# Two projection units moved among the y products, four copies moved to ScalarE, and the last group's norm applied behind its out products

## The reference

```
proj = rmsnorm(h) @ w_in                      # z, xbc, dt
xbc  = silu(dwconv5(proj_xbc))                # x, B, C
y    = scan_forward(x,B,C) + scan_backward(x,B,C) + x * d_skip
y    = y * silu(z)                            # gate
yg   = y in 4 groups of 512 channels
yg   = yg * rsqrt(mean(yg*yg) + 1e-6)         # norm of one group
h    = h + (yg * norm_w) @ w_out
```

## Time and profile before

| what | value |
|---|---|
| median of 3 runs | 1836.99 us (1836.5 to 1837.8) |
| the profiled execution's own time | 1833.54 us |
| its span, first to last instruction | 1831.8 us |
| PE busy | 1578.1 us, 86% |
| DVE busy | 1282.2 us, 70% |
| ACT busy | 781.0 us, 43% |
| POOL busy | 165.6 us, 9% |
| TensorE clock granted, mean | 0.907 |

### The profile page before, as it was taken

One profiled execution on the slowest core, in us unless ns is written; L12 is line 12 of the kernel. 1 busy time (PEld: TensorE's weight loads), 2 busy tenths in 40 slices (PEclk: granted clock), 3 DMA queues, 4 the chain that ended last, 5 costly groups with the idle time before them and its releaser, 6 DMA issues.

```text
span 1831.8 us, 20798 instructions
## 1 busy us (share of the span) xinstructions
PE 1578.1 (86%) x7275; PEld 1269.4 (69%) x7275; DVE 1282.2 (70%) x1673; ACT 781.0 (43%) x1323; POOL 165.6 (9%) x200
## 2 busy tenths in 40 slices
PE   3984987987985799999998777887898999999996
PEld 1753756755754588778877556887686888888875
DVE  4577766866875676696679898997466677663355
ACT  3348465473473455513442322221234555542242
POOL 1153000000000450000001020000010000000000
PEclk7987998998997899999999986675899999999998
DMA  2233313303320523252334564662232323333231
GB/s 71 82 92 117 92 46 115 105 33 118 112 70 23 114 87 97 81 184 92 102 133 161 191 240 143 162 166 53 66 104 70 102 92 100 95 97 104 90 94 64
DMA packets 189607, 190.57 MB, mean 104 GB/s; under 512 B 47566, under 2 KB 178206, under 8 KB 185438
## 3 DMA queue, kind: packets, MB, share of 16 engines
q1 hardware_dynamic: 168926, 187.52, 32.4%
q10 hardware_dynamic: 20608, 2.10, 0.9%
HBM read 165.27 MB, written 24.31 MB: 103 GB/s over the span
## 4 chain that ended last, share of the span: by engine, by line
PE 59%; DVE 25%; ACT 9%; issue 4%; DMA 2%; ACTq 1%; SPq 1%; DVEq 0%
PE ring L1829 19%; PE ring L1830 18%; PE ring L1831 18%; ACT rows L992 3%; ACT rows L1002 3%; DVE w_lo L1224 2%; DVE rb L1631 2%; DMA rows<-log_decays 1%; DVE ul L1238 1%; PE pe_y L1972 1%; DVE cc L1348 1%; DVE s_prod L1590 1%; DVE tab L1551 1%; DVE ytmp L1502 1%; DVE rstd L1247 1%
## 5 line engine op out<-in xcount | busy, mean ns | idle before, releaser
L879 ACT ACTIVATE w_hi<-w_raw 128x1024 fp32r<-128x1024 f32 (+1 forms) x233 | 239.9, 1029 | 656.7 <-PE ring L1831 626.2
L1829 PE MATMUL ring<-uh,w_hi 128*128 128x512 f32 (+1 forms) x1160 | 461.9, 398 | 36.5 <-DVE w_lo L1224 30.1
L1830 PE MATMUL ring<-ul,w_hi 128*128 128x512 f32 (+1 forms) x1160 | 455.7, 393 | 0.0
L1831 PE MATMUL ring<-uh,w_lo 128*128 128x512 f32 (+1 forms) x1160 | 455.0, 392 | 0.0
L1224 DVE TENSOR_TENSOR w_lo<-w_raw,w_hi 128x1024 fp32r<-128x1024 f32 (+1 forms) x233 | 278.0, 1195 | 188.4 <-ACT w_hi L879 188.2
L1829 PEld LDWEIGHTS ring<-uh,w_hi 128*128 128x128 f32 (+1 forms) x1160 | 220.1, 190 | 94.7 <-DVE w_lo L1224 25.7
L1830 PEld LDWEIGHTS ring<-ul,w_hi 128*128 128x128 f32 (+1 forms) x1160 | 220.1, 190 | 47.3 <-issue 2.1
L1831 PEld LDWEIGHTS ring<-uh,w_lo 128*128 128x128 f32 (+1 forms) x1160 | 219.7, 189 | 47.4 <-issue 0.6
L1829 PE MATMUL ring<-gh,w_hi 128*128 128x512 f32 x480 | 190.5, 397 | 29.2 <-DVE w_lo L1224 16.1
L1830 PE MATMUL ring<-gl,w_hi 128*128 128x512 f32 x480 | 189.1, 394 | 0.0
L1831 PE MATMUL ring<-gh,w_lo 128*128 128x512 f32 x480 | 189.0, 394 | 0.0
(11 more groups left out here) (250 smaller groups left out, 2173.9 us busy)
## 6 DMA issues: line engine op xcount, KB each, us to landing
w_raw<-in_ffn_w_up SPq DMA_DIRECT2D x88, 512.0 KB, 3.5
w_raw<-in_ffn_w_down SPq DMA_DIRECT2D x40, 512.0 KB, 3.5
w_raw<-in_ssd_w_in SPq DMA_DIRECT2D x32, 512.0 KB, 4.4
rows<-log_decays SPq DMA_DIRECT2D x16, 1024.0 KB, 5.9
s_tables<-tab SPq DMA_DIRECT2D x16, 1024.0 KB, 6.2
slot<-s_tables SPq DMA_DIRECT2D x16, 1024.0 KB, 7.4
w_raw<-in_ssd_w_out SPq DMA_DIRECT2D x16, 512.0 KB, 3.5
w_raw<-in_ple_w_gate SPq DMA_DIRECT2D x16, 512.0 KB, 3.5
```

The costliest lines, as they stand in the source:

```text
L879: act.activation(w_hi[u % 2][:, 0:n], w_raw[:, u % 2, 0:n], ACT.Copy).then_inc(hi_done, 1)
L1829: pe.matmul(o, wh[:, k, c], rh[:, k0 + k, :], start=first and k == 0, stop=False)
L1830: pe.matmul(o, wh[:, k, c], rl[:, k0 + k, :], start=False, stop=False)
L1831: mm_ = pe.matmul(o, wl[:, k, c], rh[:, k0 + k, :], start=False, stop=last and k == nk - 1)
```

## The change

1. **Units of the next group among the y** (PE). In g = 0, 1 and 2 the two first xbc units of group g+1 are multiplied inside the y stage of g instead of behind it: the list `between` gives what stands ahead of `transposes(hp+1)` (or, for hp = 3, ahead of `outputs(3)`), and what stands after the last `outputs`. The second of the two units stands behind `outputs(3)` and ahead of `group_square(g)`. The loop over xbc of groups 1 to 3 begins with its third unit.
2. **x and B copies on ACT**. The four `xseq` copies and the `bseq` copy go from DVE to ACT, behind `hi_to(z + 3)` and ahead of the silu of z.
3. **The last group** (g = 3). y times `norm_w` alone is split into `yh_last` and `yl_last` inside the y stage, pair by pair: DVE `y_normed` and `y_rest`, ACT `y_hi` behind the decays that are due in that step. Its own out products follow without the norm; `group_square` comes after the first of them, and each pair of result tiles is multiplied by `ytmp` into a buffer `part` and then added to `h` (`take_last_out`: four DVE instructions in place of two). The out units 2 and 3 of group 2 move later in the y stage (`between[3]`), with their `hi`, `lo` and `take_out`.

```diff
--- before.py
+++ after.py
@@ -176,6 +176,10 @@
         bseq = sb("bseq", [P, SB, P], where=ssd)
         cb_fwd = sb("cb_fwd", [P, SEQ], where=ssd)
         zs = sb("zs", [P, GT, SEQ], where=ssd)
+        last_y = ExitStack()
+        yh_last = sb("yh_last", [P, GT, SEQ], F32R, last_y)
+        yl_last = sb("yl_last", [P, GT, SEQ], F32R, last_y)
+        last_y.close()
         xd = sb("xd", [P, 2, GC], where=ssd)
         car = sb("car", [P, 2, SB - 1, GC], where=ssd)
         yo = sb("yo", [P, SB, GC], where=ssd)
@@ -196,6 +200,7 @@
         speq = rows_[0][0:2 * HEADS, 0, 0, :]
         cs_row = rows_[1][0:2 * HEADS, 0, 0, :]
         ssd.close()
+        YH, YL = [yh] * (GROUPS - 1) + [yh_last], [yl] * (GROUPS - 1) + [yl_last]
 
         def ffn_memory(layer, where):
             m = ExitStack()
@@ -361,6 +366,7 @@
         y5_skip, y5_gelu = sem("s5_skip_added"), sem("s5_gelu")
         g5_hi, g5_lo = sem("g_hi"), sem("g_lo")
         glu_sig, glu_mul = sem("glu_sigmoid"), sem("glu_product")
+        out_scaled = sem("out_scaled")
         hn_done = sem("h_normed")
         stored = sem("output_stored")
 
@@ -969,6 +975,12 @@
                         act.wait_ge(taps, 8 * (3 * g + i) + 6 + j + 1)
                         act.activation(dst, cc[:, q % 4, :], ACT.Silu).then_inc(silu, 1)
                 hi_to(z + 3)
+                for c in range(SB + 1):
+                    name, k = (("xseq", g), c) if c < SB else (("bseq", g), 0)
+                    act.wait_ge(evac, T[name] + k)
+                    act.wait_ge(filled, FILL[name] + k + 1)
+                    dst = xseq[:, c, :] if c < SB else bseq[:].rearrange("p c n -> p (c n)")
+                    act.activation(dst, bank(T[name] + k), ACT.Copy).then_inc(evac, 1)
                 for i in range(2):
                     if i == 1:
                         if g == 0:
@@ -1006,10 +1018,19 @@
                 if g:
                     hi_to(w + 2)
                 decays(1)
+                def y_hi(m):
+                    act.wait_ge(yn_done, GT * g + m + 1)
+                    act.activation(YH[g][:, m, :], zs[:, m, :], ACT.Copy).then_inc(yh_done, 1)
+
                 for hp in range(GT + 1):
                     if hp + 2 < GT:
                         decays(hp + 2)
-                    if hp + 1 < GT and g:
+                    if g == GROUPS - 1:
+                        if hp:
+                            y_hi(hp - 1)
+                        if hp in (0, 2, 4):
+                            hi_to(w + 3 + hp // 2)
+                    elif hp + 1 < GT and g:
                         hi_to(w + hp + 3)
                     if hp >= 1:
                         n = GT * g + hp - 1
@@ -1023,11 +1044,10 @@
                 act.activation(var[:], var[:], ACT.Sqrt).then_inc(gstd, 1)
                 if g < GROUPS - 1:
                     hi_to(U[("xbc", g + 1)] + 2)
-                if g:
-                    act.wait_ge(unit_done, w + 4)
-                for m in range(GT):
-                    act.wait_ge(yn_done, GT * g + m + 1)
-                    act.activation(yh[:, m, :], zs[:, m, :], ACT.Copy).then_inc(yh_done, 1)
+                    if g:
+                        act.wait_ge(unit_done, w + 4)
+                    for m in range(GT):
+                        y_hi(m)
             for i in range(4):
                 hi_to(U[("out", GROUPS - 1)] + i + 2)
                 for m in (2 * i, 2 * i + 1):
@@ -1372,10 +1392,7 @@
                 take_z(0)
                 lo_to(z + 3)
 
-                for c in range(SB):
-                    take(("xseq", g), c, xseq[:, c, :])
-                dve.wait_ge(filled, FILL[("bseq", g)] + 1)
-                dve.tensor_copy(bseq[:], bank(T[("bseq", g)]).rearrange("p (c n) -> p c n", c=SB)).then_inc(evac, 1)
+                dve.wait_ge(evac, T[("cb", g)])
                 dve.wait_ge(filled, FILL[("cb", g)] + 1)
                 cb_ = bank(T[("cb", g)]).rearrange("p (c l) -> p c l", c=SB)
                 for d, m in ((0, le), (1, ge)):
@@ -1485,16 +1502,44 @@
                         dve.tensor_tensor(yo[:, c, :], yo[:, c, :], ytmp[:], ALU.add).then_inc(yo_add, 1)
                         adds += 1
 
+                def y_normed(m, factor):
+                    if factor is None:
+                        op = dve.tensor_scalar(zs[:, m, :], xT[:, m, :], col(C_SSDN + GT * g + m), None, ALU.mult)
+                    else:
+                        op = dve.scalar_tensor_tensor(out=zs[:, m, :], in0=xT[:, m, :], scalar=col(C_SSDN + GT * g + m),
+                                                      in1=factor, op0=ALU.mult, op1=ALU.mult)
+                    op.then_inc(yn_done, 1)
+
+                def y_rest(m):
+                    dve.wait_ge(yh_done, GT * g + m + 1)
+                    dve.tensor_tensor(YL[g][:, m, :], zs[:, m, :], YH[g][:, m, :].bitcast(F32), ALU.subtract
+                                      ).then_inc(yl_done, 1)
+
                 for hp in range(GT):
                     weigh(hp)
-                    if g:
-                        lo_to(w + hp + 2)
+                    if g and (g, hp) != (GROUPS - 1, 2):
+                        lo_to(w + hp + 2 - (g == GROUPS - 1 and hp == 3))
                     add_yoff(hp)
                     if hp:
                         finish(hp - 1)
-                    if hp + 1 < GT and g:
+                    if 0 < g < GROUPS - 1 and hp + 1 < GT:
                         take_out(g - 1, hp + 1)
+                    if g == GROUPS - 1:
+                        if hp:
+                            dve.wait_ge(gated, GT * g + hp)
+                            y_normed(hp - 1, None)
+                        if hp in (0, 2):
+                            take_out(g - 1, 1 + hp // 2)
+                        if hp:
+                            y_rest(hp - 1)
                 finish(GT - 1)
+                if g == GROUPS - 1:
+                    dve.wait_ge(gated, GT * GROUPS)
+                    y_normed(GT - 1, None)
+                    y_rest(GT - 1)
+                if g == GROUPS - 1:
+                    take_out(g - 1, 3)
+                    lo_to(w + 5)
 
                 dve.wait_ge(gsq_used, 2 * g + 2)
                 dve.tensor_scalar(var[:], pe_s[:], 1.0 / GC, EPS, ALU.mult, ALU.add).then_inc(gvar, 1)
@@ -1503,16 +1548,27 @@
                 dve.wait_ge(grstd, g + 1)
                 if g < GROUPS - 1:
                     lo_to(U[("xbc", g + 1)] + 2)
-                for m in range(GT):
-                    dve.wait_ge(gated, GT * g + m + 1)
-                    dve.scalar_tensor_tensor(out=zs[:, m, :], in0=xT[:, m, :], scalar=col(C_SSDN + GT * g + m),
-                                             in1=ytmp[:], op0=ALU.mult, op1=ALU.mult).then_inc(yn_done, 1)
-                for m in range(GT):
-                    dve.wait_ge(yh_done, GT * g + m + 1)
-                    dve.tensor_tensor(yl[:, m, :], zs[:, m, :], yh[:, m, :].bitcast(F32), ALU.subtract
-                                      ).then_inc(yl_done, 1)
+                    for m in range(GT):
+                        dve.wait_ge(gated, GT * g + m + 1)
+                        y_normed(m, ytmp[:])
+                    for m in range(GT):
+                        y_rest(m)
+
+            def take_last_out(i):
+                t = T[("out", GROUPS - 1, i)]
+                part = rows_[0][:, 0].rearrange("p j l -> p (j l)").rearrange("p (j l) -> p j l", j=2)
+                dve.wait_ge(unit_done, U[("out", GROUPS - 1)] + i + 1)
+                if i:
+                    dve.wait_ge(evac, t)
+                for j in range(2):
+                    dve.tensor_tensor(part[:, j, :], bank(t + j), ytmp[:], ALU.mult).then_inc(out_scaled, 1)
+                for j in range(2):
+                    dve.wait_ge(out_scaled, 2 * i + j + 1)
+                    dve.wait_ge(evac, T[("out", GROUPS - 2, i)] + j + 1)
+                    dve.tensor_tensor(h[:, 2 * i + j, :], h[:, 2 * i + j, :], part[:, j, :], ALU.add).then_inc(evac, 1)
+
             for i in range(4):
-                take_out(GROUPS - 1, i)
+                take_last_out(i)
                 lo_to(U[("out", GROUPS - 1)] + i + 2)
                 for m in (2 * i, 2 * i + 1):
                     u_lo(1, m, uh0, ul0)
@@ -1901,14 +1957,16 @@
                                 last=kg == 1)
 
                 def out_product(g, i):
-                    product(U[("out", g)] + i, T[("out", g, i)], GT, 0, yh, yl)
+                    product(U[("out", g)] + i, T[("out", g, i)], GT, 0, YH[g], YL[g])
+
+                def xbc_product(g, i, kg):
+                    product(U[("xbc", g)] + 2 * i + kg, T[("xbc", g)] + 2 * i, 4, 4 * kg, uh0, ul0, first=kg == 0,
+                            last=kg == 1)
 
                 u = U[("xbc", g)]
-                for i in range(3):
+                for i in range(g > 0, 3):
                     for kg in range(2):
```

(26 more changed lines are left out.)

## The result

The median is 1842.39 us after (20 runs, 1838.97 to 1849.84) and 1837.17 us before (20 runs, 1833.48 to 1841.46). The ratio is 1.0031 with an interval of 1.0023 to 1.0039: the changed kernel is slower by 5.2 us. The forecast was 1837.9, no difference, in a range of 1831 to 1843. The time lies inside the range, near its top; the sign was not forecast, and "slower by over 0.2%" had been given a chance of 0.24 against 0.51 for "within".

What follows compares the result with a forecast made beforehand. The prediction read the chain that ended last, PE holding 59% and DVE 25%, with either as the bound at each place. Its terms, +3.1 - 3.6 - 3.0 + 3.75 - 3.1 + 3.75 = +0.9, took 1836.99 to 1837.9 us, range 1831 to 1843.

Steps and rivals of the forecast that it cites:

- Copies on ACT, group 0: Five copies ahead of the silu of z delay the dt steps and the first decay: +3.1 us.
- Copies on ACT, groups 1 to 3: z's second product starts 1.2 us earlier per group and everything behind it follows: -3.6 us in all.
- Units among the y: From `outputs(2)` to the sums of squares, one unit stays in the chain: -1.5 us each in groups 1 and 2, -3.0.
- The third unit's slow start: Behind PE's idle 6 us the third unit may take 7.7 instead of 5.4 us; hidden, or up to 2 us per group.
- Last group, y stage: `weigh(2)` on DVE queues behind `y_rest(0)`, which waits for ACT's `y_hi(0)`, so `outputs(3)` comes later: +3.75 us.
- From `outputs(3)` to the first result tile: In the last group this stretch takes 21.17 instead of 24.30 us: -3.1.
- Evacuation: Last group's result tiles: four DVE instructions per pair instead of two, first pair 5.6 instead of 5.44, others +1.2 each: +3.75 us.
- A: Passage between groups: PE, not the chain over DVE, sets it; three units of 5.5 go; 1824.4 us, chance 0.07.
- B: Last group: `weigh(2)` not held and doubled evacuation hidden behind out products, each 0 instead of +3.75; 1830.4 us, chance 0.17.
- C: Evacuation: a DVE SBUF add beside a POOL sum takes 1.74 instead of 0.6; +4.5 more, 1842.4 us, chance 0.15.
- D: ACT's copies begin no earlier, or PE waits for something else: 0 instead of -3.6, +3.1 kept; 1841.5 us, chance 0.08.

Runs made afterwards that it cites:

- part 3 alone: The kernel before with only the last group's norm moved behind its out products: 1842.63 against 1835.14 us, ratio 1.0037.
- mended: Kernel before plus only the last group's change, with `y_rest` one pair later (ratio 1.0020), then also sums of squares, variance and reciprocal earlier (0.9995).
- without its scaling: Kernel before plus only the last group's change, leaving out the multiplication by `ytmp`: 1836.37 against 1836.90 us, ratio 0.9999.
- the rearranged unit: Kernel before plus only the moved xbc units, the second behind the sums of squares in groups 0 to 2: 1823.64 against 1836.90 us, ratio 0.9933.

## Why the prediction held in most steps and missed in the sum

**Copies on ACT, group 0: right.** +3.38 against +3.1. The copies were priced at 0.57 and took 0.61 to 0.63. Leaving group 0 out gave 3.1 us back by the medians, 2.0 by the ratios.

**Copies on ACT, groups 1 to 3: right for the place, wrong for what follows.** Three times 1.0 instead of 1.2 at z's product. The step that failed is the sentence "Everything behind z's product (states, decays) follows it". Behind it stands a wait of 3.13 us in front of the second pair of states. Twelve kernels have that wait in three groups each, 36 passages, and it was 3.13 us in all. In the 17 where those four matmuls took 2.88 us or less, z's product to `outputs(0)` took 42.63 to 42.72. In the 19 where they took 3.27 to 3.78, it took 43.58 to 44.27, but for one (42.61). Over all 42 passages of the fourteen kernels the granted clock of the stretch sorts them without exception: 0.96 in all with 42.61 to 42.72 us, 0.92 in all with 43.58 to 44.27, and 1.00 in the one passage of 41.09, which has the unread matmuls. The five kernels that are as the kernel before up to this place (itself and the four with part 3 alone, mended or without its scaling) have none of the second kind in 15 passages; the seven that have part 1 or 2 have 19 in 21. So either part, moving the stages in front of this wait, cost some 1.2 us in nearly every group at a place that it did not touch: 2.35 in the changed kernel, which was struck in two groups of three. With three unread matmuls in the wait the clock held behind it in all six passages. The prediction had asked of PE's idle time only what stood behind the sums, not behind this wait.

The parts don't add in the totals. Alone they come to 3.3 (all copies), 1.3 (units) and 6.8 us (last group) by the ratios, 11.4 together against the whole's 5.2. Up to the variance of the FFN's norm the traces have them at +3.62, -1.70 and +5.49, 7.41 together, against +6.28 for the whole (613.89 before, 617.51, 612.19 and 619.38 alone, 620.17 together). Part of what is left there can be the loss at the states, which both of the first two have alone (3.2 and 2.3 us) and the whole has once, at 2.35. The larger part of the gap is in the totals alone: behind the mixer, where none of the parts changes anything and the rest of the span still varied from 1217.9 to 1224.6 us between the traces, and the intervals of the three ratios are 2 to 3 us wide either way. It stays open.

**Units among the y: right in the chain, in part by luck in the sum.** -2.76 against -3.0; one unit stayed in the chain, and PE's wait behind the sums was 6.09 for a forecast of some 6. But `outputs(3)` to variance gave 1.86 and 1.89 us, more than the 1.5 each of the forecast, and group 2's y stage took 1.1 of it back: from `outputs(2)` to `outputs(3)`, with the moved unit between, it took 9.88 us there at a granted clock of 0.71, 8.60 in group 1 at 0.84; 9.14 was forecast. The third unit's slow start was hidden. What I did not ask is the better question: why should the unit stand in front of the sums at all? The order of two calls took the ratio from 1.0007 to 0.9933, 13.6 us.

**Last group, y stage: right.** +4.13 against +3.75; DVE's `weigh(2)` did stand behind the wait for ACT's copy of y, and moving `y_rest` one pair later brought the stage from 32.97 to 29.83.

**From `outputs(3)` to the first result tile: right.** -3.41 against -3.1.

**Evacuation: the mechanism right, the size wrong.** +5.44 against +3.75. The multiplications were 1.2 per pair, as worked out. The first pair cost 0.47 more than before, forecast was 0.16 (5.6 for 5.44): of the 1.0 us of waits that I took for room, 0.73 was. And the end of the stage was not DVE's: the last sums of squares on PE took 3.78 instead of 2.26, and DVE waited 1.34 for them. "PE has its products ready by then" was true and was the trouble: having them ready it stood idle (3.05 and 1.87 us) in front of the sums that the variance needs. Without the scaling, PE idle for 0.49 and 0.68 us, they took 2.26. The granted clock was 0.50 over the slow ones and 1.00 over those before the change; this stretch is the larger part of the miss, 1.34 of 1.69.

**The rivals.** A failed, since DVE's chain sets the passage; even the rearranged unit gave 12.3 of the 16.5 us that it priced. B failed: neither the head start nor a hidden evacuation is there. C hit the time (1842.4) by luck, for another reason. Its price was an SBUF add beside a POOL sum; its "2.1 us per pair of now" is 1.9 in the trace (3.47 for a pair of `ul` beside POOL, 1.54 without). POOL's timeline shows its sums, which run beside the pairs of `ul`, as before:

```profile
602.57 3.84 POOL L701 TENSOR_TENSOR var<-var,sq 128x512 f32<-128x512 f32 x2 [3.09 <-ACT sq L901]
609.51 3.78 POOL L701 TENSOR_TENSOR var<-var,sq 128x512 f32<-128x512 f32 x2 [3.10 <-ACT sq L901]
```

The new adds end at 602.4 and 609.4, before each of them begins, so their contention was never tested here; each took 0.64 as elsewhere. D failed for the copies by themselves (z's product did get earlier), but its total (1841.5) came close: at the states 2.35 of the copies' 3.04 was lost again.

**The range.** The forecast's own 1834.4 to 1841.4 is 3.5 us either way, and the bounds of its terms give more: added, they reach from -8 to +10 us around the kernel before, and the evacuation, which missed by most, had no bounds. That 1842.4 lies in the stated range is due to what the rivals C and D added to it.

**Two rules.** The Trainium skill's page "VectorE: DVE Perf Modes", section "Mode 2×_2P — use both read ports for one tensor", says that a float32 op with a scalar on one SBUF tensor runs twice as fast; from that came the estimate of 0.3 us for `y_normed`. The row at 563.83 has it at 0.49, and the next instruction starts 0.40 behind it, where a two-input op's does 0.6 to 0.7 behind: less than twice as fast, nearer to the page than to my 0.6. With the exclusive lock in the Trainium skill's page "SBUF — State Buffer", section "SBUF: two separate sides", the `ul` pairs agree (3.48 us beside a POOL sum, 1.53 at 617.30 without one); on the new adds no run here shows it.

## What to carry to other kernels

Where a reduction ends a chain over other engines, put it ahead of any independent unit and let the unit fill the wait: the order of two calls was worth 13.6 us here, where the three parts of the change together lost 5. Before a wait is put into an engine's queue, list what stands behind it, and let that which doesn't need the wait go first. A gain in front of a PE wait of some 3 us isn't passed on as a matter of course: read the granted clock behind the wait in both kernels, and see whether there is work, even unread work, to put into it.

## What the runs showed of the hardware

The same wait of 3.13 us in front of the same four matmuls left the granted clock at 1.00 in one kernel (382 to 386 before, though in group 1 of the same kernel the four took 2.79 us instead of 2.33) and at 0.67, 0.62 or 0.50 in others, whose stages in front were only some us shorter or longer. Three matmuls that nobody reads, put into the wait so that 0.56 us was left of it, kept the states at 2.33 us in all six passages of two kernels; the first of the two went from 1.0007 to 0.9975 with them, each against the kernel before. Over the stretch of some 43 us behind z's product, a granted clock of 1.00, 0.96 and 0.92 went with 41.1, 42.6 to 42.7 and 43.6 to 44.3 us. What in the work ahead of the wait decides whether the clock falls isn't settled by these runs.

ACT's copy of a 128x512 float32 tile out of PSUM runs at 0.62 us a tile (2.48 for four), as DVE's did (2.48 for four).
